# A diffusion step in fp32: the gate rows summed in four chunks, and a first modulation block of two tiles

## The chip, the core and the metric

One core of one Trainium2 chip runs the whole program. The metric is the device time of one execution in microseconds; the runs shown are three executions, and one further execution was taken by the hardware profiler. All times inside the kernel are from that profiled execution, counted from its first instruction.

## The reference

One layer of a trunk on 5 tiles of 128 tokens: one tile of context (the prompt), four of latent tokens. All in float32, D_MODEL = 2048.

```python
mod = silu(cond) @ w_ada + b_ada                 # 2048 x 6144, for two conditions: latent, context
shift, scale, gate = split(mod, 3)
h = rms_norm(x, g_norm) * (1 + scale) + shift
z = h @ w_in                                     # q, k, v, gates of both mixers
oa = diff_attention(...)                         # 8 heads: softmax 1 - lam * softmax 2
ob = gqa_attention(...)                          # 8 query heads on 2 key/value heads
o = concat(rms_norm(oa, subln) * silu(ga), ob * silu(gb)) @ w_out
x = x + gate * o
y = rms_norm(x, g_final)                         # also out: new keys and values of the context
```

The three thirds of w_ada are 16 MB each. Shift and scale are needed before the first projection, gate only after the last one.

## The kernel before

Products run on TensorE in float32 split into a high and a low part (fp32r): each 128 x 512 product is three matmuls, high x high, low weight x high, high weight x low (lines 588 to 590). A step is one block of 128 rows of a weight times the five token tiles, fifteen matmuls into the five banks of z_ps. Sixteen steps are a pass, which yields 512 output columns for all tokens. There are 17 passes: pass 0 for the keys and values of the grouped mixer (KV), passes 1 to 4 (G_IT on) for two grouped query heads each, passes 5 to 12 (D_IT on) for one differential head each, passes 13 to 16 (OUT_IT on) for w_out. Between the tiles of a pass stand pieces of the attention of the group that the pass before projected: QK transposes, scores S, transposes T of the probabilities, products V, transposes O of the output (STEPS, pieces_at). They use three PSUM banks, `ring`.

Weights arrive in w_raw (two pairs of row blocks), ScalarE copies them to w_hi, VectorE makes w_lo (split_w, line 1189) three steps ahead of TensorE. VectorE works in the order of its own program: in each step first split_w, then the attention's parts, and at the end of the step what belongs to the gate. TensorE waits for w_lo, and, for V and S, for pt_lo (line 1291), which frees or completes the probabilities. In the output passes VectorE multiplies z_ps by the gate rows (gated_y), adds x (add_x) and weighs by g_final (weight_y); the last pass finishes tile by tile.

Modulation. Shift and scale come in blocks of tiles of 128 columns, ADA_TILES. A block of n tiles is loaded in 2n loads of 1 MB into a ring of six buffers (ada_raw); a buffer is reloaded when its matmuls are done. TensorE multiplies each load by the conditions (modulation, line 610, sixteen or thirty-two small matmuls), VectorE copies the rows (modulation_rows), TensorE transposes them (columns, line 625), and VectorE makes the factors (modulation_columns). Block 0 comes before pass 0, the others between the tiles of pass 0 in slots given by ada_pieces: five slots a step. Step s of pass 0 needs the factors of tile s.

The gate third is not multiplied on TensorE as a matrix. VectorE forms sums over the sixteen row blocks of w_ada, weighted per partition (gate_sums, line 1390: acc = raw * cs + acc, for two conditions), and one small matmul group per 512 columns then adds over the partitions (step_gate, line 812). VectorE adds b_ada (gate_rows_out), GpSimd stores the rows to DRAM and loads them back, broadcast to 128 partitions, as gate_b for each output pass. The sums are 64 pieces of two instructions on 512 columns, ten a pass in passes 6 to 12:

```python
GATE_STEPS = [4, 4, 9, 9, 11, 11, 13, 13, 13, 13]
```

The group of matmuls follows step 0 of pass 13, the stores its step 3, and gate_b is loaded with x_add at step 10 of pass 13 and at step 1 of passes 14 to 16. Order is kept by semaphores alone; each engine's instructions stand in the order in which its function issues them.

## Time and profile before

| | us |
|---|---|
| median of the 3 runs shown | 1325.59 (1324.25 to 1325.9) |
| the profiled execution | 1323.39 |
| its span, first to last instruction | 1321.6 |
| TensorE busy | 1249.9 |
| VectorE busy | 799.8 |
| ScalarE busy | 607.0 |
| GpSimd busy | 245.0 |
| DMA | 156.54 MB |

The first matmul of pass 0 starts at 50.05, and the last instructions end 11 us after TensorE. Over the first 120 us the DMA engines are full, afterwards they move about 100 GB/s. The mean granted clock of TensorE is 0.991 of full speed; the share of a single stretch is in the rows. A busy share near one does not say that TensorE runs at its peak: matmuls overlap, and at the lower clock they are as busy and slower. So the waits and the clock of single stretches are to be read, not the share.

### The profile page before, as it was taken

Reading aid. Unit: us, or ns where it says so; the run is one execution under the profiler, and the core shown is the slowest. Engines: PE = TensorE matmul, PEld = TensorE weight load, DVE = VectorE, ACT = ScalarE, POOL = GpSimd, SP = SyncE. Lnnn points to the kernel's source line nnn. Section 1 sums busy time; section 2 is a strip of 40 time slices with the busy share of each in tenths; the row PEclk is TensorE's granted clock in tenths of the full one; section 3 lists DMA queues with packets and bytes.
Section 4 is the critical chain, followed back from the end, with each engine's and each line's share of the span. In section 5 each row is a group of like instructions: output and inputs, shape, how many; then the busy total and the mean of one; then the engine's idle time right before and its main releaser. Section 6 shows DMA issues by size and latency. Waiting matters only on the chain.

```text
span 1321.6 us, 18198 instructions
## 1 busy us (share of the span) xinstructions
PE 1249.9 (95%) x6903; PEld 1009.5 (76%) x6903; DVE 799.8 (61%) x1283; ACT 607.0 (46%) x1275; POOL 245.0 (19%) x426
## 2 busy tenths in 40 slices
PE   3899999999999999999999999999999899999996
PEld 1456778888888888887777787777777777888885
DVE  3344637657466565676767767677777776523343
ACT  4223325545545464464545445454545656322123
POOL 2010102002020040222222222222223232200001
PEclk9899999999999999999999999999999999999999
DMA  9998422112121121334243242323334331433234
GB/s 352 386 376 258 104 65 74 38 49 84 49 68 49 48 93 48 106 87 125 77 127 98 81 120 78 110 83 121 98 95 139 104 101 64 151 120 135 80 136 160
DMA packets 130904, 156.54 MB, mean 118 GB/s; under 512 B 8008, under 2 KB 98216, under 8 KB 130048
## 3 DMA queue, kind: packets, MB, share of 16 engines
q1 hardware_dynamic: 118032, 111.22, 25.7%
q0 software_dynamic: 12784, 44.15, 10.5%
q8 instruction: 55, 0.90, 0.3%
q14 instruction: 33, 0.27, 0.1%
HBM read 144.18 MB, written 11.16 MB: 118 GB/s over the span
## 4 chain that ended last, share of the span: by engine, by line
PE 81%; DVE 10%; ACT 2%; issue 2%; DMA 2%; POOL 1%; SPq 0%; ACTq 0%; DVEq 0%; POOLq 0%
PE z_ps L588 21%; PE z_ps L590 20%; PE z_ps L589 20%; PE ring L786 4%; PE ring L685 4%; DVE gate_acc L1390 3%; PE ring L720 3%; PE ring L610 2%; PE ring L788 2%; DVE w_lo L1189 1%; DMA ada_raw<-in_w_ada_dram 1%; DVE pt_lo L1291 1%; PE ring L590 1%; PE ring L589 1%; PE ring L588 1%
## 5 line engine op out<-in xcount | busy, mean ns | idle before, releaser
L588 PE MATMUL z_ps<-w_hi,xt_hi 128*128 128x512 f32 x1360 | 564.8, 415 | 8.4 <-DVE xt_lo L1183 7.4
L590 PE MATMUL z_ps<-w_hi,xt_lo 128*128 128x512 f32 x1360 | 533.6, 392 | 0.0
L589 PE MATMUL z_ps<-w_lo,xt_hi 128*128 128x512 f32 x1360 | 533.0, 392 | 0.0
L860 ACT ACTIVATE w_hi<-w_raw 128x512 fp32r<-128x512 f32 x272 | 170.5, 628 | 349.4 <-PE z_ps L590 338.4
L1189 DVE TENSOR_TENSOR w_lo<-w_raw,w_hi 128x512 fp32r<-128x512 f32 x272 | 191.5, 706 | 225.7 <-ACT w_hi L860 223.7
L588 PEld LDWEIGHTS z_ps<-w_hi,xt_hi 128*128 128x128 f32 x1360 | 257.0, 189 | 66.3 <-issue 20.8
L590 PEld LDWEIGHTS z_ps<-w_hi,xt_lo 128*128 128x128 f32 x1360 | 256.6, 189 | 57.0
L589 PEld LDWEIGHTS z_ps<-w_lo,xt_hi 128*128 128x128 f32 x1360 | 258.1, 190 | 39.3
L786 PE MATMUL ring<-v_hl,pt_hi 128*128 128x256 f32 x400 | 96.8, 326 | 14.8 <-DVE pt_lo L1291 13.9
L1266 DVE TENSOR_REDUCE small<-s_sb 128x2 f32<-128x1536 f32 (+1 forms) x60 | 87.9, 1466 | 23.5 <-ACT s_sb L860 22.6
L860 ACT ACTIVATE o_sum<-ring 128x128 f32<-128x128 f32 (+1 forms) x60 | 18.8, 314 | 178.2 <-PE ring L788 178.2
L967 ACT ACTIVATE s_sb<-s_sb,small 128x768 f32<-128x768 f32 (+1 forms) x120 | 97.9, 819 | 2.5 <-DVE small L1266 2.4
L786 PEld LDWEIGHTS ring<-v_hl,pt_hi 128*128 128x128 f32 x400 | 75.2, 188 | 20.5 <-issue 17.6
L788 PE MATMUL ring<-v_hl,pt_lo 128*128 128x128 f32 x400 | 89.1, 223 | 0.0
L860 ACT ACTIVATE pt_hi<-ring 128x256 fp32r<-128x256 f32 (+2 forms) x144 | 66.6, 467 | 47.0 <-PE ring L685 45.9
L1560 POOL TENSOR_TENSOR sg<-sg,zs 128x128 f32<-128x128 f32 (+1 forms) x60 | 36.6, 610 | 276.4 <-DVE sg L1249 275.8
L1291 DVE TENSOR_TENSOR pt_lo<-ring,pt_hi 128x256 fp32r<-128x256 f32 (+2 forms) x144 | 73.2, 523 | 21.4 <-ACT pt_hi L860 18.9
L1390 DVE SCALAR_TENSOR_TENSOR gate_acc<-gate_raw,cs,gate_acc 128x512 f32<-128x512 f32 x120 | 83.6, 761 | 0.2 <-issue 0.2
L788 PEld LDWEIGHTS ring<-v_hl,pt_lo 128*128 128x128 f32 x400 | 76.4, 191 | 2.8
L1302 DVE TENSOR_TENSOR o_sum<-ring,o_sum 128x128 f32<-128x128 f32 (+1 forms) x60 | 20.0, 333 | 87.1 <-ACT o_sum L860 87.1
L1249 DVE RECIPROCAL sg<-sg 128x128 f32<-128x128 f32 (+1 forms) x60 | 72.5, 1209 | 0.0
L685 PE MATMUL ring<-ident,s_sb 128*128 128x128 f32 x400 | 66.3, 272 | 0.0
(154 smaller groups left out, 1310.5 us busy)
## 6 DMA issues: line engine op xcount, KB each, us to landing
w_raw<-in_w_in_dram SPq DMA_DIRECT2D x192, 256.0 KB, 3.2
ada_raw<-in_w_ada_dram SPq DMA_DIRECT2D x64, 512.0 KB, 11.7
gate_raw<-in_w_ada_dram POOLq DMA_DIRECT2D x32, 512.0 KB, 4.7
w_raw<-in_w_out_dram SPq DMA_DIRECT2D x64, 256.0 KB, 3.5
o_spill<-row_st POOLq DMA_DIRECT2D x14, 320.0 KB, 3.1
row_st<-o_spill POOLq DMA_DIRECT2D x14, 320.0 KB, 3.4
x_sb<-in_x_sample_dram SPq DMA_DIRECT2D x4, 1024.0 KB, 10.2
w_raw<-in_w_in_dram POOLq DMA_DIRECT2D x16, 256.0 KB, 6.4
```

Source lines behind the costliest of these rows:

```text
L588: pe.matmul(out, hi_l, hi_r, start=start, stop=False)
L589: pe.matmul(out, hi_l, lo_r, start=False, stop=False)
L590: return pe.matmul(out, lo_l, hi_r, start=False, stop=stop)
L685: return pe.transpose(bank[:, col:col + P], src, ident[:, :])
L786: pe.matmul(bank[:, o:o + 2 * DH], pt_hi[c_][:, keys], v_hl[vh][:, vt, :], start=(j == 0), stop=False, skip_group_check=True)
L788: ins = pe.matmul(bank[:, o:o + DH], pt_lo[c_][:, keys], v_hl[vh][:, vt, 0:DH], start=False, stop=(j == tiles[-1][0]), skip_group_check=True)
L860: return act.activation(out, in_, ACT.Copy, **kw)
L967: act.activation(row, row, ACT.Exp, bias=nmax[:, t, c_:c_ + 1], accum_out=den[:, t, c_:c_ + 1]).then_inc(exp_done, 1)
L1189: dve.tensor_tensor(w_lo[:, b, :], w_raw[:, kg // 2 % RAW_RING, kg % 2, :], w_hi[:, b, :].bitcast(F32), ALU.subtract).then_inc(w_lo_done, 1)
L1266: dve.tensor_reduce(nmax[:, t, :], s_sb[:, t % 2, :, 0:(NKEY if t else P)], AX_X, ALU.max, negate=True).then_inc(max_ready, 1)
L1291: ins = dve.tensor_tensor(pt_lo[c_][:, keys], RB(n)[:, col:col + P * w], pt_hi[c_][:, keys].bitcast(F32), ALU.subtract)
L1390: ins = dve.scalar_tensor_tensor(acc, raw, weight, acc, ALU.mult, ALU.add)
```

## The change

Three things change.

1. The gate's columns are cut in four chunks of 512, one per output pass. Chunk 0 is summed in pass 1 (steps 4 to 7 and 9 to 12), chunks 1 to 3 in the output pass that ends with them, passes 14 to 16 (steps 1 to 5 and 7 to 9). A step takes two row blocks, four instructions on 512 columns. The raw rows come in loads of 512 KB for chunk 0 and 1 MB for the others, in two buffers each. Every chunk has its own group of small matmuls (now on 128 columns), adds, stores and broadcast: chunk 0 at steps 0 to 3 of pass 2, the others at steps 10 to 12 of their pass. Nothing of the gate is left in passes 5 to 13 but the load of gate_b for chunk 0. The eight loads of b_ada move from pass 5 to pass 1, and the computation of lambda (minus_lambda) from step 8 to step 13 of pass 1.
2. ADA_TILES is 2, 4, 4, 4, 2 instead of 4, 4, 4, 2, 2. Four loads come before pass 0 instead of eight, and 28 groups of matmuls lie in pass 0 instead of 24.
3. The columns of a block are transposed one slot earlier, and VectorE makes its factors in the step in which it copies the rows, a step earlier than before.

```diff
-GATE_COLS = D_MODEL // 2
-GATE_LOADS = 2 * KT
-GATE_STEPS = [4, 4, 9, 9, 11, 11, 13, 13, 13, 13]
-GATE_FROM = 4
-GATE_SUM_IT = OUT_IT
-ADA_TILES = [4, 4, 4, 2, 2]
+GATE_EARLY = [4, 5, 6, 7, 9, 10, 11, 12]
+GATE_LATE = [1, 2, 3, 4, 5, 7, 8, 9]
+ADA_TILES = [2, 4, 4, 4, 2]
...
-def gate_parts():
-    out, i = {}, 0
-    for it in range(D_IT + 1, GATE_SUM_IT):
-        for s in GATE_STEPS:
-            if i < 2 * GATE_LOADS and (it, s) >= (D_IT + 1, GATE_FROM):
-                out.setdefault((it, s), []).append(i)
-                i += 1
-    return out
-GATE_PARTS = gate_parts()
+def gate_steps(cc):
+    return G_IT if cc == 0 else OUT_IT + cc, GATE_EARLY if cc == 0 else GATE_LATE
+def gate_unit(cc, k):
+    n = 2 if cc == 0 else 4
+    return (k // n if cc == 0 else KT // 2 + (cc - 1) * (KT // 4) + k // n), n
+GATE_SUMS, GATE_SUM_AT, GATE_ROWS_AT, GATE_OUT_AT, GATE_LOADS = {}, {}, {}, {}, {}
+for _cc in range(OUTS):
+    _it, _steps = gate_steps(_cc)
+    for _i, _s in enumerate(_steps):
+        GATE_SUMS[(_it, _s)] = (_cc, _i)
+    _n = gate_unit(_cc, 0)[1]
+    for _q in range(KT // _n):
+        _s = _steps[(_q - 1) * _n // 2 - 1] + 1 if _q >= 2 else 2 if _cc == 0 else 0
+        GATE_LOADS.setdefault((_it, _s), []).append((_cc, _q))
+    GATE_SUM_AT[(G_IT + 1, 0) if _cc == 0 else (_it, 10)] = _cc
+    GATE_ROWS_AT[(G_IT + 1, 0) if _cc == 0 else (_it, 11)] = _cc
+    GATE_OUT_AT[(G_IT + 1, 3) if _cc == 0 else (_it, 11)] = _cc
...
-            i = (e + 1) * (slots - 6) // ADA_LOADS[c] - 1
+            i = max((e + 1) * (slots - 8) // ADA_LOADS[c] - 1, 0)
             out.setdefault(divmod(TILES * ADA_FIRST[c - 1] + i, TILES), []).append(("ADA", c, e))
-        out.setdefault(divmod(TILES * ADA_FIRST[c] - 5, TILES), []).append(("COLS", c, 0))
+        out.setdefault(divmod(TILES * ADA_FIRST[c] - 6, TILES), []).append(("COLS", c, 0))
...
-    gate_raw, e = place("gate_raw", [P, 2, GATE_COLS], F32, half0)
-    gate_acc, e = place("gate_acc", [P, 2, D_MODEL], F32, e)
-    gate_sel, e = place("gate_sel", [P, 2, 2], F32, e)
...
+    gate_raw0, e0 = place("gate_raw0", [P, 2, 2, NCOL], F32, e)
+    gate_acc0, e0 = place("gate_acc0", [P, 2, NCOL], F32, e0)
...
+    gate_raw1, e0 = place("gate_raw1", [P, 2, 4, NCOL], F32, e0)
+    gate_acc1, e0 = place("gate_acc1", [P, 2, NCOL], F32, e0)
...
-            def step_gate():
-                n = TURN["GATE"]
+            def step_gate(cc):
+                n = TURN[("GATE", cc)]
                 bank = claim(n)
                 pe.wait_ge(sel_set, 4)
-                pe.wait_ge(gate_summed, 2 * GATE_LOADS)
+                pe.wait_ge(gate_summed, KT * (cc + 1))
+                acc = gate_acc1 if cc else gate_acc0
                 for r in range(2):
                     for j in range(4):
-                        ins = pe.matmul(bank[32 * j:32 * j + 2, :], gate_sel[:, r, :],
-                                        gate_acc[:, r, NCOL * j:NCOL * (j + 1)], start=(r == 0), stop=(r == 1))
+                        ins = pe.matmul(bank[32 * j:32 * j + 2, 0:P], gate_sel[:, r, :], acc[:, r, P * j:P * (j + 1)],
+                                        start=(r == 0), stop=(r == 1))
                 filled(ins, n)
             for e in range(2):
                 modulation(0, e)
             for g in range(HT_GROUPS):
                 h_transposes(g)
-                modulation(0, 2 + g)
-            for e in range(2 + HT_GROUPS, ADA_LOADS[0]):
-                modulation(0, e)
+                if g < 2:
+                    modulation(0, 2 + g)
             columns(0)
...
+                if a == G_IT:
+                    wait_full(act, TURN[("GATE", 0)])
...
-                    if it == G_IT and s == KT // 2:
+                    if it == G_IT and s == KT - 3:
...
-            def gate_sums(i):
-                m, piece = divmod(i, 2)
-                k, u = divmod(m, 2)
-                dve.wait_ge(gate_in[u], 16 * (k + 1))
-                if k:
-                    dve.wait_ge(gate_summed, i - 3)
-                raw = gate_raw[:, u, NCOL * piece:NCOL * (piece + 1)]
-                c0 = GATE_COLS * u + NCOL * piece
-                for r in range(2):
-                    acc, weight = gate_acc[:, r, c0:c0 + NCOL], cs[:, KT * r + k:KT * r + k + 1]
-                    if k == 0:
-                        ins = dve.tensor_scalar(acc, raw, weight, None, ALU.mult)
-                    else:
-                        ins = dve.scalar_tensor_tensor(acc, raw, weight, acc, ALU.mult, ALU.add)
-                ins.then_inc(gate_summed, 1)
+            def gate_sums(cc, i):
+                for k in (2 * i, 2 * i + 1):
+                    g, n = gate_unit(cc, k)
+                    raw, acc = (gate_raw1, gate_acc1) if cc else (gate_raw0, gate_acc0)
+                    dve.wait_ge(gate_in[g % 2], 16 * (g // 2 + 1))
+                    if k:
+                        dve.wait_ge(gate_summed, KT * cc + k)
+                    elif cc:
+                        wait_full(dve, TURN[("GATE", cc - 1)])
+                    for r in range(2):
+                        src, weight = raw[:, g % 2, k % n, :], cs[:, KT * r + k:KT * r + k + 1]
+                        if k == 0:
+                            ins = dve.tensor_scalar(acc[:, r, :], src, weight, None, ALU.mult)
+                        else:
+                            ins = dve.scalar_tensor_tensor(acc[:, r, :], src, weight, acc[:, r, :], ALU.mult, ALU.add)
+                    ins.then_inc(gate_summed, 1)
...
-                        if s + 1 in ADA_FIRST:
-                            modulation_columns(ADA_FIRST.index(s + 1))
                         split_h(s + 1)
                         if s + 2 in ADA_FIRST:
                             modulation_rows(ADA_FIRST.index(s + 2))
+                            modulation_columns(ADA_FIRST.index(s + 2))
...
-                    if (it, s) == (GATE_SUM_IT, 1):
-                        gate_rows_out()
-                    for i in GATE_PARTS.get((it, s), []):
-                        gate_sums(i)
+                    if (it, s) in GATE_SUMS:
+                        gate_sums(*GATE_SUMS[(it, s)])
+                    if (it, s) in GATE_ROWS_AT:
+                        gate_rows_out(GATE_ROWS_AT[(it, s)])
...
+            def load_gate_rows(cc):
+                pool.wait_ge(gate_out, 64 * (cc + 1))
+                if cc:
+                    pool.wait_ge(y_add, TILES * cc)
                 for r in range(2):
-                    pool.dma_start(gate_b[:, r, :], gate_rows[r:r + 1, cols].broadcast_to([P, NCOL])
+                    pool.dma_start(gate_b[:, r, :], gate_rows[r:r + 1, NCOL * cc:NCOL * (cc + 1)].broadcast_to([P, NCOL])
                                    ).then_inc(gate_b_in, 16)
-            def load_gate(m):
-                k, u = divmod(m, 2)
-                c0 = 2 * D_MODEL + GATE_COLS * u
-                pool.dma_start(gate_raw[:, u, :], ada_v[k, :, c0:c0 + GATE_COLS]).then_inc(gate_in[u], 16)
-            def gate_begin():
-                pool.wait_ge(og_ready, OG_DONE[D_IT - 1])
-                for m in range(2):
-                    load_gate(m)
-                for r in range(2):
-                    pool.memset(gate_sel[:, r, r:r + 1], 1.0).then_inc(sel_set, 1)
-                    pool.memset(gate_sel[:, r, 1 - r:2 - r], 0.0).then_inc(sel_set, 1)
+            def load_gate(cc, q):
+                g, n = gate_unit(cc, (2 if cc == 0 else 4) * q)
+                if (cc, q) == (0, 0):
+                    for r in range(2):
+                        pool.memset(gate_sel[:, r, r:r + 1], 1.0).then_inc(sel_set, 1)
+                        pool.memset(gate_sel[:, r, 1 - r:2 - r], 0.0).then_inc(sel_set, 1)
+                if (cc, q) == (1, 0):
+                    for u in range(2):
+                        wait_full(pool, TURN[("O", OUT_IT - 1, 0)] + u)
+                if q >= 2:
+                    pool.wait_ge(gate_summed, KT * cc + n * (q - 1))
+                elif cc:
+                    pool.wait_ge(gate_summed, KT * cc)
+                c0 = 2 * D_MODEL + NCOL * cc
+                pool.dma_start((gate_raw1 if cc else gate_raw0)[:, g % 2, :, :], ada_p[:, n * q:n * (q + 1), c0:c0 + NCOL]
+                               ).then_inc(gate_in[g % 2], 16)
...
-                    if (it, s) == (D_IT, 4):
+                    if (it, s) == (G_IT, 4):
+                        pool.wait_ge(qk_ready, G_IT)
+                        bias = b_ada[:, 2 * D_MODEL:].rearrange("a (c j n) -> a c j n", c=OUTS, j=4)
                         for j in range(4):
                             for r in range(2):
-                                c0 = 2 * D_MODEL + 512 * j
-                                pool.dma_start(ada_rows[32 * j + r:32 * j + r + 1, :], b_ada[:, c0:c0 + 512]
-                                               ).then_inc(gate_bias, 16)
-                    if (it, s) == (GATE_SUM_IT, 3):
-                        wait_free(pool, TURN["GATE"])
+                                pool.dma_start(ada_rows[32 * j + r:32 * j + r + 1, :].rearrange("p (c n) -> p c n", c=OUTS),
+                                               bias[:, :, j, :]).then_inc(gate_bias, 16)
+                    if (it, s) in GATE_LOADS:
+                        for cc, q in GATE_LOADS[(it, s)]:
+                            load_gate(cc, q)
+                    if (it, s) in GATE_OUT_AT:
+                        cc = GATE_OUT_AT[(it, s)]
+                        wait_free(pool, TURN[("GATE", cc)])
                         for j in range(4):
-                            pool.dma_start(gate_rows[:, 512 * j:512 * (j + 1)], ada_rows[32 * j:32 * j + 2, :]
+                            c0 = NCOL * cc + P * j
+                            pool.dma_start(gate_rows[:, c0:c0 + P], ada_rows[32 * j:32 * j + 2, P * cc:P * (cc + 1)]
                                            ).then_inc(gate_out, 16)
...
                     if it == OUT_IT and s == 10:
-                        pool.wait_ge(gate_out, 64)
                         load_out_operands(0)
+                        load_gate_rows(0)
...
+                    if it > OUT_IT and s == 12:
+                        load_gate_rows(it - OUT_IT)
```

At TensorE's start (names: ada_raw holds w_ada, x_sb the normalized x, z_ps the projection) stood, before:

```order
L638 MATMUL ring<-ident,x_sb 128x128 x16
L644 MATMUL ring<-ident,x_sb 128x128 x4
L610 MATMUL ring<-ada_raw,cs 2x256 x24
L625 MATMUL ring<-ident,ada_rows 128x128 x2
L588 MATMUL z_ps<-w_hi,xt_hi 128x512
L589 MATMUL z_ps<-w_lo,xt_hi 128x512
L590 MATMUL z_ps<-w_hi,xt_lo 128x512
L610 MATMUL ring<-ada_raw,cs 2x256 x8
```

and stands now:

```order
L649 MATMUL ring<-ident,x_sb 128x128 x16
L655 MATMUL ring<-ident,x_sb 128x128 x4
L636 MATMUL ring<-ident,ada_rows 128x128
L599 MATMUL z_ps<-w_hi,xt_hi 128x512
L600 MATMUL z_ps<-w_lo,xt_hi 128x512
L601 MATMUL z_ps<-w_hi,xt_lo 128x512
L621 MATMUL ring<-ada_raw,cs 2x256 x56
L599 MATMUL z_ps<-w_hi,xt_hi 128x512
L600 MATMUL z_ps<-w_lo,xt_hi 128x512
L601 MATMUL z_ps<-w_hi,xt_lo 128x512
L621 MATMUL ring<-ada_raw,cs 2x256 x8
```

Block 0 ends with the transposes and one transpose of its rows; all of block 1 but one load follows the first tile of step 0.

On VectorE, at step 13 of pass 7 (pt_lo is what the V matmuls of TensorE wait for), stood, before:

```order
L1189 TENSOR_TENSOR w_lo<-w_raw,w_hi 128x512
L1302 TENSOR_TENSOR o_sum<-ring,o_sum 128x128
L1390 SCALAR_TENSOR_TENSOR gate_acc<-gate_raw,cs,gate_acc 128x512 x8
L1189 TENSOR_TENSOR w_lo<-w_raw,w_hi 128x512
L1291 TENSOR_TENSOR pt_lo_64<-ring,pt_hi_63 128x512
L1291 TENSOR_TENSOR pt_lo_64<-ring,pt_hi_63 128x256
L1319 SCALAR_TENSOR_TENSOR og<-o_sum,small,sg 128x128
L1189 TENSOR_TENSOR w_lo<-w_raw,w_hi 128x512
```

and stands now:

```order
L1203 TENSOR_TENSOR w_lo<-w_raw,w_hi 128x512
L1316 TENSOR_TENSOR o_sum<-ring,o_sum 128x128
L1203 TENSOR_TENSOR w_lo<-w_raw,w_hi 128x512
L1305 TENSOR_TENSOR pt_lo_64<-ring,pt_hi_63 128x512
L1305 TENSOR_TENSOR pt_lo_64<-ring,pt_hi_63 128x256
L1333 SCALAR_TENSOR_TENSOR og<-o_sum,small,sg 128x128
L1203 TENSOR_TENSOR w_lo<-w_raw,w_hi 128x512
```

The eight sums between o_sum and the next split weight are gone; nothing took their place.

On VectorE in pass 1, from step 4 to the k_lo of step 8 (gate_acc_84 and gate_raw_83 are chunk 0's), stood, before:

```order
L1189 TENSOR_TENSOR w_lo<-w_raw,w_hi 128x512 x6
L1162 TENSOR_TENSOR lam_raw_72<-lam_raw_72 128x512
L1162 TENSOR_TENSOR lam_raw_73<-lam_raw_73 128x512
L1164 TENSOR_REDUCE lam<-lam_raw_72 128x8
L1164 TENSOR_REDUCE lam<-lam_raw_73 128x8
L1171 TENSOR_TENSOR lam<-lam 128x8
L1172 TENSOR_SCALAR lam<-lam 128x8
L1257 TENSOR_TENSOR k_lo_61<-ring,k_hi_60 128x512
L1257 TENSOR_TENSOR k_lo_68<-ring,k_hi_67 128x512
```

and stands now:

```order
L1203 TENSOR_TENSOR w_lo<-w_raw,w_hi 128x512 x2
L1404 TENSOR_SCALAR gate_acc_84<-gate_raw_83,cs 128x512 x2
L1406 SCALAR_TENSOR_TENSOR gate_acc_84<-gate_raw_83,cs,gate_acc_84 128x512 x2
L1203 TENSOR_TENSOR w_lo<-w_raw,w_hi 128x512
L1406 SCALAR_TENSOR_TENSOR gate_acc_84<-gate_raw_83,cs,gate_acc_84 128x512 x4
L1203 TENSOR_TENSOR w_lo<-w_raw,w_hi 128x512
L1406 SCALAR_TENSOR_TENSOR gate_acc_84<-gate_raw_83,cs,gate_acc_84 128x512 x4
L1203 TENSOR_TENSOR w_lo<-w_raw,w_hi 128x512
L1406 SCALAR_TENSOR_TENSOR gate_acc_84<-gate_raw_83,cs,gate_acc_84 128x512 x4
L1203 TENSOR_TENSOR w_lo<-w_raw,w_hi 128x512
L1271 TENSOR_TENSOR k_lo_61<-ring,k_hi_60 128x512
L1271 TENSOR_TENSOR k_lo_68<-ring,k_hi_67 128x512
```

The lambda work ahead of k_lo has gone to step 13, and sixteen sums stand ahead of it instead, four after each split weight.

## Rows read from the trace of the kernel before

**Rows 1.** The page's part 1: engine, busy us (share of the span) xinstructions.
```profile
...
PE 1249.9 (95%) x6903; PEld 1009.5 (76%) x6903; DVE 799.8 (61%) x1283; ACT 607.0 (46%) x1275; POOL 245.0 (19%) x426
...
```

**Rows 2.** Waits of TensorE, passes 6 to 12: total us, times, longest.
```profile
...
PE ring L786 <- DVE pt_lo L1291: 13.9, 6, 2.5
PE ring L720 <- DVE pt_lo L1291: 8.2, 6, 3.2
PE ring L786 <- ACT s_sb L860: 0.9, 1, 0.9
```

**Rows 3.** Timeline of VectorE, passes 7, 12: start us, us, instruction [idle before].
```profile
...
675.27 5.38 DVE L1390 SCALAR_TENSOR_TENSOR gate_acc<-gate_raw,cs,gate_acc 128x512 f32<-128x512 f32 x8
...
681.17 1.01 DVE L1291 TENSOR_TENSOR pt_lo<-ring,pt_hi 128x512 fp32r<-128x512 f32 x2
...
1040.66 2.73 DVE L1390 SCALAR_TENSOR_TENSOR gate_acc<-gate_raw,cs,gate_acc 128x512 f32<-128x512 f32 x4
...
```

**Rows 4.** TensorE by stretch: length, busy us (xinstructions), granted clock, DMA share, GB/s.
```profile
...
682.00:688.00 6.00, 5.56 (x23) 0.72 0.74 229
759.00:765.00 6.00, 5.28 (x29) 1.00 0.78 235
...
```

**Rows 5.** Waits of TensorE in passes 0 and 1.
```profile
...
PE z_ps L588 <- DVE xt_lo L1183: 3.9, 4, 1.1
PE ring L685 <- DVE k_lo L1257: 2.9, 1, 2.9
...
```

**Rows 6.** Timeline of TensorE around the gate step of pass 13.
```profile
...
1074.01 1.90 PE L812 MATMUL ring<-gate_acc,gate_sel 128*2 128x512 f32 x16
...
```

**Rows 7.** Timeline of all engines at the start.
```profile
...
5.19 109.82 SPq L554 DMA_DIRECT2D ada_raw<-in_w_ada_dram  x64
...
41.37 2.89 PE L610 MATMUL ring<-ada_raw,cs 128*2 128x256 f32 x48
...
44.34 1.72 DVE L1124 COPY ada_rows<-ring 2x256 f32<-2x256 f32 x4 [0.36 <-PE ring L610]
...
50.05 0.77 PE L588 MATMUL z_ps<-w_hi,xt_hi 128*128 128x512 f32 x1 [3.44 <-DVE xt_lo L1183]
...
61.14 1.05 PE L610 MATMUL ring<-ada_raw,cs 128*2 128x256 f32 x16
...
```

**Rows 8.** Instructions on ada_raw up to 130 us; DMA from issue to landing.
```profile
...
L610 PE MATMUL ring<-ada_raw,cs x632: 272/379/634, 20.5 to 130.0; 128*2 128x256 f32 x96, 128*2 128x128 f32 x62
...
DMA to landing us min/median/max: 7.8/11.7/16.2
```

**Rows 9.** Timeline of VectorE in pass 14.
```profile
...
1175.11 0.69 DVE L1189 TENSOR_TENSOR w_lo<-w_raw,w_hi 128x512 fp32r<-128x512 f32 x1 [2.71 <-ACT w_hi L860]
```

**Rows 10.** Timeline of VectorE at step 8 of pass 1.
```profile
...
171.69 1.41 DVE L1162 TENSOR_TENSOR lam_raw<-lam_raw 128x512 f32<-128x512 f32 x2
...
175.38 1.29 DVE L1257 TENSOR_TENSOR k_lo<-ring,k_hi 128x512 fp32r<-128x512 f32 x2 [0.18 <-ACT k_hi L860]
...
```

**Rows 11.** Instructions on gate_raw: DMA from issue to landing.
```profile
...
DMA to landing us min/median/max: 3.8/4.7/6.8
```

**Rows 12.** Timelines of ScalarE and VectorE at the end.
```profile
...
1293.44 0.63 ACT L860 ACTIVATE w_hi<-w_raw 128x512 fp32r<-128x512 f32 x1 [2.77 <-PE z_ps L590]
...
1299.61 0.69 DVE L1353 TENSOR_TENSOR y_sb<-z_ps,gate_b 128x512 f32<-128x512 f32 x1 [1.40 <-PE z_ps L590]
...
1312.46 3.02 ACT L860 ACTIVATE y_sb<-y_sb,stat 128x1536 f32<-128x1536 f32 x2
...
```

**Rows 13.** DMA issues: engine op xcount, KB each, median us to landing.
```profile
...
w_raw<-in_w_in_dram SPq DMA_DIRECT2D x192, 256.0 KB, 3.2
...
gate_rows<-ada_rows POOLq DMA_DIRECT2D x4, 4.0 KB, 3.1
...
```

**Rows 14.** Instructions on lam_raw: DMA from issue to landing.
```profile
...
DMA to landing us min/median/max: 4.1/6.0/7.2
```

**Rows 15.** Waits of TensorE from pass 13 on.
```profile
...
PE ring L720 <- DVE pt_lo L1291: 0.4, 1, 0.4
```

35 lines of the change are left out of this document (15 added, 20 removed).

## The prediction, written before the changed kernel was run

> **What bounds the kernel now.** I read the page first, then the waits of TensorE, then the timelines around each wait. TensorE is busy 1249.9 of 1321.6 us [rows 1], so time can only be won where it starts late, waits or runs at the lower clock. In the stretch of passes 6 to 12 it waits 13.9 us in six places at line 786 and 8.2 us in six places at line 720, always for VectorE's pt_lo, and 0.9 us once for ScalarE [rows 2]. In front of that pt_lo VectorE's timeline shows the gate sums: 5.38 us for the eight at step 13, 2.73 us for the four at step 9 [rows 3]. The clock comes on top: after the wait at 682 the six microseconds have a granted clock of 0.72, after the equal wait at 760 it is 1.00 [rows 4]; 0.72 means that part of the stretch ran at the lower of the two levels, 1.2 instead of 2.4 GHz. The windows at 835 and 1045 read like the one at 682, those at 606, 912 and 988 like the one at 759. Each low window costs 6 x 0.28 = 1.7 us. In passes 0 and 1 the waits are 3.9 us (four, at the first tile of each modulation block) and 2.9 us (one, for k_lo) [rows 5].
>
> **The differential passes.** All gate sums leave passes 6 to 12. The six waits at line 786: ahead of the pt_lo at 681.17 stood 5.38 us of sums; TensorE waited 2.3 us, so VectorE is now ready 3 us early and the wait is gone: -13.9. At line 720 the usual wait is 1.0 us against 2.7 us of sums, gone too. The longest, 3.2 us in pass 12, has 2.73 us of sums before it [rows 3], and 0.5 us stay: -7.7. Of the 0.9 us for ScalarE I count 0.4, since it comes after a chain that also held sums. The three low-clock windows follow such waits and go with them: -5.1. Sum -27.1. Bounds: -28.1 if all goes, -11 if ScalarE or another wait takes half the places. What is late next is ScalarE's pt_hi, but pt_lo is held by the sums in VectorE's own order, not by it. The bias loads leave pass 5 and their 2 KB cost nothing at either place.
>
> **The gate step.** One group of sixteen records on 512 columns took 1.90 us on TensorE [rows 6]. Now there are four on 128 columns; the nearest row, 16 records of 256 columns, took 1.05 us [rows 7]. Half of that and a change of operands give 0.7 us each, 2.8 us together: +0.9. Bounds +0.2 (0.5 each) and +2.3 (1.05 each).
>
> **Start and pass 0.** The same 32 modulation groups run, but 28 instead of 24 lie inside pass 0. (a) The first matmul at 50.05 follows the last transposes, three split weights, the rows' copy and the columns; the three groups at 41.37 ran beside VectorE's work, not ahead of it [rows 7]. Only one group between the transposes (about 1 us) and half of the copies leave the path: -1.4, not the 4.2 us of four groups. (b) Four more groups in the pass: seven now stand in a row in the first slot (1.0 us each), the other 21 cost 1.05 us and a change of operands, some 1.2: 32.2 us against 24 x 1.2 = 28.8: +3.4. (c) VectorE computes the columns one step earlier, so the waits at the blocks' first tiles, 3.9 us [rows 5], go; the transposes of the rows keep theirs: -3.6. Sum -1.6. Against it stands the ring of six loads: loads 10 and 11 are issued only once the first groups of block 1 have run, at about 51 and 53 us, and loads take at least 7.8 us to land in this crowd [rows 8], less when the queue has run dry. Block 1's last group is due at about 60, so I expect no wait, and at the end there is room: the last issue is at 115.0, the last group at 130.0 [rows 7, 8]. Bounds -5 and +6 (two loads that land 3 us late, each time at the lower clock).
>
> **Pass 1.** VectorE gets 32 sums there. Two rows of w_ada cost 2.73 us [rows 3] and the wait on the sum just before, some 0.1 each: 2.9; with a split weight's 0.6 that is 3.5 us per step, and a step of TensorE takes 3.4 (a w_lo of 0.69 us and 2.71 us idle to the next, [rows 9]). The split weights are made three steps ahead, 10 us of cover, so being 1 us behind costs nothing. It matters only at step 8, where TensorE waits 2.9 us for k_lo [rows 5]: before, the lambda work (from 171.69 to 175.2) stood in front of k_lo at 175.38 [rows 10]. It moves to step 13, where nothing waits. In its place VectorE comes late from steps 4 to 7: the third and fourth pairs of w_ada rows are loaded only once the first two are summed, 4.7 us from issue to landing [rows 11] against the 3.5 us until they are wanted, so each such round loses about 1 us. I get k_lo at 175.7 on the old scale: +0.5. GpSimd's queue meets eight bias loads there, ahead of the third load; they are through before the first sum. Bounds -2.5 and +5. In pass 2 the four adds for the gate rows come before q_lo, some 0.3 us each (copies of twice the width took 1.72 us for four [rows 7]); q_lo waits for ScalarE in part, so +0.3.
>
> **The output passes.** There VectorE gets 32 sums in each of three. It starts step 1 with ten operations on y just done (0.6 to 0.7 us each, [rows 12]), needs 3.5 us a step for nine steps (at step 6 the weighing of y stands in place of sums), and is some 5 us behind all along. The split weights, at the head of each step, are then about 2 us later than now, of 10. The gate step of step 10 needs the last sum at about 1 us before TensorE gets there. Loads of 1 MB are issued a pass ahead or two steps ahead. So 0, bounds 0 and +6 (2 us at each gate step).
>
> **The tail.** Before, the last gate rows were in SBUF well before they were wanted. Now chunk 3 is summed in pass 16 itself, and its chain starts when TensorE has done step 10, at T = 1293.4 on the old scale [rows 12]: gate step 0.7; split weight and four adds to T+2.5; four stores of 0.5 us each, the last issued at T+4.2 and landed 3.1 us later [rows 13], T+7.3; then two broadcasts of 256 KB, 0.5 us apart. Four of that shape, for lam_raw, landed after 4.1 to 7.2 us, median 6.0 [rows 14]; for the second of two I take 5.5: T+13.4. But since TensorE finishes the last pass tile by tile, its first tile is ready at T+6.2 (1299.61) [rows 12]. VectorE therefore starts 6.5 us late and catches up while ScalarE becomes the chain: per tile 0.8 us of squares and 1.5 us of scaling (3.02 for two [rows 12]), 5 x 2.3 = 11.5 us after T+14.8, and about 0.5 us of waits: T+26.8. Now it ends at 1315.48 = T+22.1. That is +4.7, of which 0.7 is the gate step's: +4.0. Bounds 0 and +7.
>
> The Trainium skill, "DMA: Bandwidth & Descriptors" (section "Anatomy of one DMA — SWDGE (gpsimd) path"), prices one DMA at a fixed 2.0 us and its bytes at 436 GB/s, thus 2.6 us for 256 KB. By that rule the last gate rows would be there at T+10.5 and the tail would cost +1.1 instead of +4.0. This case's broadcasts of the same shape took 4.1 us at least and 6.0 us in the median [rows 14], so the measurement decides.
>
> **Sum.** -27.1 + 0.9 - 1.6 + 0.5 + 0.3 + 0 + 4.0 = -23.0. The profiled execution took 1323.4 us (span 1321.6), so 1300.4; the median of the runs shown, 1325.6, is 2.2 us above it, and on that scale I forecast 1302.6 us.
>
> **Rivals.**
> Cheap tail: the last broadcasts, alone on the queues, land in about 3 us, as plain loads of 256 KB do (3.2 us, [rows 13]). For it: lam_raw's four went beside other transfers. Then the sum is -25.9, 1299.7 us. This is what the skill's rule above would make of it. Chance 0.17.
> Starved start: with four groups' worth of loads consumed and the ring full, the DMA queues idle until TensorE reaches block 1, and later groups wait for their loads, in a pass in which loads are issued up to 115.0 and take 7.8 to 16.2 us to land [rows 7, 8]. Some 6 us more: about 1309. Against it: the last group has 7 us in hand. Chance 0.13.
> Half the waits stay: something else is as late as the sums, 22.1 + 5.1 us of waits and clock shrink only by half: +13, 1316. Against it: the equal steps of pass 13, without sums, have only one wait for pt_lo, of 0.4 us [rows 15]. Chance 0.08.
> The other side: VectorE as the new bound. In pass 1 and passes 14 to 16 it works 3.5 us in a step of 3.4, and two loads in flight serve two units of sums. If the loads come late, TensorE first uses up the 10 us of cover and then waits in every step, and its clock falls as at 682. With steps of s us a pass loses 8 (s - 3.4) - 10 us: as slow as before from s = 5.4 on (4 x 6 = 24 us). Steps of 6 us, landings of 9 us in pass 1 as in the crowd of pass 0 [rows 8], would cost 4 x 10.8 us and some 8 us of clock: about 1354. Against it: gate loads have landed in 3.8 to 6.8 us [rows 11]. Chance 0.04.
> The change doesn't do what it says: a gate chunk reaches its pass late, so that the gated y of passes 14 to 16 waits at each pass start, 3 x 3 us: 1312. Against it: there T+13.4 meets a first tile at T+15.0 (gate step 0.7, four steps of 3.4, a tile of 0.7), 1.6 us of room in each pass. Chance 0.06.
>
> **How the numbers follow.** The forecast itself has 0.52. Its own bounds and the cheap tail reach down to 1295; the starved start and the late chunk reach up to 1312; half of the waits staying and VectorE as the bound are left out, about 0.12, and the rest of the 2 in 10 are sizes beyond both ends. A measurement tells 0.2%, 2.7 us, from no change. Only VectorE as the bound is slower by that: slower 0.04. Within 0.2% lie 0.02, the part of the half-waits case in which the start is starved too and the tail dear; faster 0.94.
>
> **What would show it.** No waits of TensorE for pt_lo over 0.6 us in passes 6 to 12 and a granted clock of 1.00 throughout them: the main term. The first matmul near 48.6 and pass 1 starting within 2 us of before: the start. One wait of about 3 us for k_lo in pass 1. No wait at the gate steps of the output passes. In the tail, the first gated y some 13 us after TensorE's step 10, waiting for gate_b, and ScalarE without a gap after it. The forecast is wrong if pt_lo still waits for ScalarE, if weights (w_lo) hold TensorE in passes 1 or 14 to 16, or if waits for ada_raw appear in pass 0.

## The result, and the profile of the changed kernel

The changed kernel takes 1309.86 us in the median of 4 runs (1309.45 to 1312.91), the kernel before 1325.52 beside it: ratio 0.9888, interval 0.9871 to 0.9906, 15.7 us faster. Forecast were 23 us and 1302.6 us; 1309.9 lies in the range, near its upper end. The profiled execution took 1309.45 us, its span is 1307.7, and it is 13.9 us shorter than the profiled execution of before.

I cut both profiled executions at the first matmul of each pass. The differences are the terms of the prediction (passes 3 to 5 took 250.6 us both times):

| stretch | before, us | after, us | change | predicted |
|---|---|---|---|---|
| up to the first matmul of pass 1 | 142.95 | 145.04 | +2.1 | -1.6 |
| pass 1 | 59.09 | 64.36 | +5.3 | +0.5 |
| pass 2 | 82.31 | 83.09 | +0.8 | +0.3, a gate step of 0.7 |
| passes 6 to 12 | 535.57 | 508.57 | -27.0 | -27.1 |
| pass 13 | 76.47 | 74.49 | -2.0 | -1.9 |
| pass 14 | 54.40 | 56.76 | +2.4 | a gate step of 0.7 |
| passes 15 and 16 | 108.96 | 110.52 | +1.6 | gate steps of 1.4 |
| after the last matmul | 11.25 | 14.2 | +3.0 | +4.0 |

The page's part 1, which answers [rows 1]: TensorE's busy time hardly moved; what was won were waits and slow matmuls.

```profile
PE 1247.1 (95%) x6951; PEld 1009.8 (77%) x6951; DVE 808.6 (62%) x1295; ACT 606.1 (46%) x1275; POOL 250.0 (19%) x426
```

TensorE's waits in the whole span (us in total, times, longest), those that the prediction's steps touch; the one for xt_lo is of pass 13 and stood there before, too. Against [rows 2] the 22.1 us for pt_lo in passes 6 to 12 have shrunk to 2.0, both in pass 12 and the longer of them 1.7 us (the 2.3 here hold 0.4 of pass 13, as in [rows 15]). Against [rows 5] the waits for xt_lo at the blocks' first tiles are gone, the one for k_lo went from 2.9 to 6.4 us, and there are seven waits for ada_raw beside the long one at the start. Six of them lie inside pass 0, 5.2 us in all, where there was none:

```profile
PE ring L621 <- DMA ada_raw<-in_w_ada_dram: 22.5, 8, 16.3
PE ring L696 <- DVE k_lo L1271: 6.4, 1, 6.4
...
PE ring L731 <- DVE pt_lo L1305: 2.3, 3, 1.7
PE ring L824 <- DVE gate_acc L1406: 1.5, 1, 1.5
PE z_ps L599 <- DVE xt_lo L1344: 1.0, 1, 1.0
```

TensorE by stretch (length, busy, granted clock, DMA share, GB/s). Where [rows 4] had a clock of 0.72 it is 1.00 now:

```profile
682.00:688.00 6.00, 6.00 (x33) 1.00 0.31 90
```

VectorE in pass 1, which answers [rows 10] (start, duration, what, idle before and its releaser). The first sums start late, for their load; another load is waited for at 177.53; the k_lo stands at the end of that line:

```profile
164.90 0.88 DVE L1404 TENSOR_SCALAR gate_acc<-gate_raw,cs 128x512 f32<-128x512 f32 x2 [1.10 <-DMA gate_raw<-in_w_ada_dram]
...
168.65 0.69 DVE L1203 TENSOR_TENSOR w_lo<-w_raw,w_hi 128x512 fp32r<-128x512 f32 x1 [1.33 <-ACT w_hi L871]
...
177.53 2.93 DVE L1406 SCALAR_TENSOR_TENSOR gate_acc<-gate_raw,cs,gate_acc 128x512 f32<-128x512 f32 x4 [1.30 <-DMA gate_raw<-in_w_ada_dram]
180.38 0.68 DVE L1203 TENSOR_TENSOR w_lo<-w_raw,w_hi 128x512 fp32r<-128x512 f32 x1
180.99 1.28 DVE L1271 TENSOR_TENSOR k_lo<-ring,k_hi 128x512 fp32r<-128x512 f32 x2
```

The DMA engines in that stretch, and TensorE's clock behind the wait (columns PE, PEld, DVE, ACT, POOL busy, then clock, DMA share, GB/s). They are full from 157 to 164, and the wait costs twice, since matmuls then run in part at the lower level:

```profile
157.00:164.00 7.00, 7.00 (x32) 5.79 (x32) 6.73 (x12) 0.63 (x1) 5.67 (x15) 1.00 1.00 229
...
177.00:183.00 6.00, 1.28 (x5) 1.18 (x6) 4.62 (x7) 0.34 (x1) 0.72 (x1) 0.64 0.50 132
183.00:189.00 6.00, 6.00 (x24) 4.85 (x23) 3.51 (x6) 1.28 (x3) 0.00 (x0) 0.79 0.43 152
```

VectorE in the last pass, against [rows 12]: the first gated y waits 5.6 us for gate_b, 11.6 us after TensorE's step 10 (1275.3).

```profile
1277.02 1.18 DVE L1361 TENSOR_TENSOR ada_rows<-ring,ada_rows 2x128 f32<-2x128 f32 x4
...
1286.92 0.69 DVE L1368 TENSOR_TENSOR y_sb<-z_ps,gate_b 128x512 f32<-128x512 f32 x1 [5.62 <-DMA gate_b<-gate_rows]
```

### The profile page after: what moved, and what is told of

It is laid out like the page before. It is cut to its first block, busy times and chain, and to the rows that moved or that the text cites. A ratio compares the mean times of both kernels' runs of the same rounds, so it can differ in the third digit from the quotient of the medians.

```text
span 1307.7 us, 18319 instructions
## 1 busy us (share of the span) xinstructions
PE 1247.1 (95%) x6951; PEld 1009.8 (77%) x6951; DVE 808.6 (62%) x1295; ACT 606.1 (46%) x1275; POOL 250.0 (19%) x426
## 4 chain that ended last, share of the span: by engine, by line
PE 83%; DVE 6%; DMA 5%; SPq 2%; ACT 1%; issue 1%; POOL 1%; ACTq 0%; DVEq 0%; POOLq 0%
PE z_ps L599 22%; PE z_ps L601 21%; PE z_ps L600 21%; PE ring L696 5%; PE ring L797 5%; PE ring L731 3%; DMA ada_raw<-in_w_ada_dram 3%; PE ring L799 2%; DVE gate_acc L1406 2%; PE ring L621 1%; SPq L565 1%; PE ring L601 1%; PE ring L600 1%; PE ring L599 1%; DMA w_raw<-in_w_out_dram 1%
```

## The experiments

Each ran five rounds beside the kernel before, on the chip of its group of runs. "Changed" is the changed kernel; its ratio is 0.9888 in its first measurement and 0.9902 in the second, so kernels of different groups are compared by their ratios.

| kernel | median, us | before, us | ratio, interval |
|---|---|---|---|
| gate's change alone | 1309.39 | 1324.33 | 0.9881 (0.9868 to 0.9895) |
| start alone, in before | 1328.34 | 1324.33 | 1.0029 (1.0018 to 1.0041) |
| changed, old blocks | 1305.95 | 1324.33 | 0.9855 (0.9840 to 0.9870) |
| changed, sums after k | 1308.38 | 1324.33 | 0.9874 (0.9861 to 0.9888) |
| changed, again | 1312.84 | 1325.88 | 0.9902 (0.9888 to 0.9917) |
| changed, sums split | 1309.81 | 1325.88 | 0.9881 (0.9865 to 0.9897) |
| changed, x later | 1311.68 | 1325.88 | 0.9895 (0.9879 to 0.9912) |
| changed, group earlier | 1309.85 | 1325.88 | 0.9879 (0.9864 to 0.9894) |
| changed, all repairs | 1297.41 | 1324.88 | 0.9789 (0.9775 to 0.9802) |
| before, sums spread | 1298.12 | 1324.88 | 0.9795 (0.9781 to 0.9808) |
| before, three edits | 1289.32 | 1325.41 | 0.9727 (0.9712 to 0.9741) |
| changed, groups ahead | 1306.68 | 1325.41 | 0.9866 (0.9846 to 0.9885) |

### The start

**The gate's change alone.** In the changed kernel:

```diff
-ADA_TILES = [2, 4, 4, 4, 2]
+ADA_TILES = [4, 4, 4, 2, 2]
...
```

with the slots, the columns and the place of modulation_columns as before, too.

> The gate's four chunks as in the changed kernel, but the start of the kernel before (blocks of 4, 4, 4, 2, 2 tiles, columns as before). Theory, from the changed kernel's waits for ada_raw in pass 0 (5.2 us in six places) and its longer pass 0 (95.67 against 92.90 us, with a first matmul only 0.7 earlier): the first block of two tiles costs 2.1 us rather than saving anything, so this kernel starts pass 1 at 143 instead of 145 and takes 1309.9 - 2.1 = 1307.8 us. Rival, the prediction's own count (the start is worth -1.6, and what came in pass 0 is from the gate's moved DMAs or from another execution): 1309.9 + 1.6 = 1311.5 us.

**The start alone**: the same edit the other way round, in the kernel before.

> The kernel before with the changed kernel's start alone (blocks of 2, 4, 4, 4, 2 tiles, columns one step earlier); the gate sums stay in passes 6 to 12. Theory (the new start starves for loads): 1325.5 + 2.1 = 1327.6 us, pass 1 starting near 145 with the same six waits for ada_raw. Rival (the start is worth -1.6): 1323.9 us. In both, passes 6 to 12 keep their 22 us of waits for pt_lo.

**The old blocks with the early factors**: in the changed kernel ADA_TILES = [4, 4, 4, 2, 2] and its loop ahead of pass 0, nothing else.

> The changed kernel with blocks of 4, 4, 4, 2, 2 tiles again, but with its columns one slot and its factors one step earlier. Theory: the wait of 3.9 us at the blocks' first tiles was removed by the earlier factors, and the starvation came from the block of two tiles alone; then both are gone here: 3.5 to 4 us under the kernel with the gate's change alone, so about 1304 us, pass 0 about 89.5 us long. Rival: the loads set the length of pass 0 whatever the blocks (the last lands at 122 to 127 us), and the 3.9 us turn up as waits for ada_raw: then within 1 us of the kernel with the gate's change alone, 1307 to 1308 us.

Pass 1 starts at 142.2, 145.9 and 138.8 us in the three; in seven executions with the block of two behind its first tile it lies between 145.0 and 146.8. TensorE's waits up to pass 1 follow, the start alone first, then the gate alone, then the old blocks with early factors. The longest of each line (16 us for the first load, 3.4 us for the first xt_lo) lies ahead of pass 0. Inside pass 0 the start alone waits 5.4 us for ada_raw, the gate alone never, and the old blocks 1.3 us.

```profile
PE ring L610 <- DMA ada_raw<-in_w_ada_dram: 23.0, 7, 16.5
```

```profile
PE z_ps L599 <- DVE xt_lo L1198: 7.4, 5, 3.4
```

```profile
PE ring L621 <- DMA ada_raw<-in_w_ada_dram: 18.2, 3, 16.1
...
PE z_ps L599 <- DVE xt_lo L1198: 3.4, 1, 3.4
```

In the kernel before, the start costs 4.0 us of the whole time (0.29%), of which 2.9 are there when pass 1 starts; the theory's sign is right, its size was too small. In its profile pass 1 is another 1.6 us longer than before (60.7 against 59.1): the wait for k_lo is 2.9 us as before, but here the clock fell after it (the last section shows both). In the changed kernel I expected 1307.8 without it and measured 1309.4; its ratio is 0.07 and 0.21 points under the changed kernel's two, which no single comparison resolves. The second of the two was meant to test this: if the start costs 4 us here too, it had to come out 2 to 4 us above the gate's change alone, and 0.21 points are 2.8 us. The two halves of the start work against each other: the early factors save 3.5 us (142.2 to 138.8; four of the five waits for xt_lo gone), the block of two costs more than that: with it and the early factors pass 1 starts 6 to 8 us later than with the early factors alone, and the whole time is 0.33 to 0.47 points longer, 4 to 6 us.

**Three groups ahead**, in the changed kernel:

```diff
+            for e in range(3):
+                modulation(1, e)
             columns(0)
```

The three groups are left out of pass 0.

> The changed kernel with its block of two tiles, but with the first three groups of block 1 ahead of the transposes of block 0's rows, where TensorE waits 3.8 us for VectorE's copy, instead of behind the first tile of pass 0. Their data have landed by 37.1, 39.8 and 42.5 us. Theory (starved start): in the changed kernel loads 10 and later were issued only from 52.7 us on, after an idle stretch since 38.4, because their buffers were freed by groups that stood behind the first tile; now they are issued from about 43 us on, the DMA share in 40 to 60 us goes back over 1, the waits for ada_raw near 58 to 62 us go, and three groups of 1.1 us leave pass 0: pass 1 starts at 140 to 142 instead of 145 to 146.8, 1312.8 - 4 = 1306 to 1309 us. Rival: the loads are the limit over the whole pass (last landing at 127 us in any case) and later waits for ada_raw grow by what the first lose: pass 1 starts at 144 or later, 1311 us or more.

TensorE and the DMA engines in 50 to 60 us, changed and with the groups ahead (busy, clock, DMA share, GB/s):

```profile
50.00:60.00 10.00, 8.92 (x118) 0.88 0.77 268
```

```profile
50.00:60.00 10.00, 8.77 (x90) 0.83 1.04 385
```

The buffers are now reloaded from 43.6 us on instead of 52.7, the engines stay full, the last load lands at 123.7 instead of 126.9 (122.2 before), and pass 1 starts at 142.0. Three groups of about 1 us have also left pass 0, which alone could explain the 3.0 us won. It does not: in all eight executions with the block of two tiles, this one included, TensorE's last wait for ada_raw ends when load 26 lands (counted from 0, as below), and pass 1 starts 35.5 to 35.6 us after that wait. With the groups ahead that load lands at 106.4 instead of 109.5, and pass 1 starts 3.0 us earlier. So the loads set the length of pass 0, and the starved start is shown. What stays are waits for ada_raw of 1.2 us at 58 and of 3.0 us in three places around 100; against the old blocks with early factors (138.8) the block of two still costs 3 us.

### Pass 1

**The sums after k**, **the sums split**:

```diff
-GATE_EARLY = [4, 5, 6, 7, 9, 10, 11, 12]
+GATE_EARLY = [4, 9, 10, 11, 12, 13, 14, 15]
```

The second has [4, 5, 9, 10, 11, 12, 13, 14] there, and minus_lambda (with ScalarE's part) at step 15.

> The changed kernel with chunk 0's sums at steps 4 and 9 to 15 of pass 1 instead of 4 to 7 and 9 to 12, so that only one of eight steps of sums stands ahead of the k_lo of step 8. Theory: the 6.4 us wait for k_lo and the low clock behind it (granted 0.64 and 0.79 in 177 to 189, some 1.7 us) are VectorE's lateness from the sums, and with lambda gone from there too the wait falls under 1 us: 1309.9 - 7 = 1303 us. Rival: k_lo waits for ScalarE's k_hi or for the w_raw loads that land late beside the broadcasts for lambda; then 2.5 us or more of the wait stay, 1306 to 1307 us. A third: the last sums at step 15 make the gate step of pass 2 wait or w_lo late, some 2 us back.

> The changed kernel with chunk 0's sums at steps 4, 5 and 9 to 14 of pass 1, and the lambda work at step 15. Moving all but one step of sums behind the k_lo freed 8.4 us in pass 1, but the last sums at step 15 ended at 208.99 and TensorE's gate step of pass 2 waited for them, 4.2 us and the lower clock after it. Theory: with steps 6 and 7 free VectorE is on time for k_lo (it has w_lo made by 174.3, k_hi is ready at 174.5), and the sums end a step earlier, at 205.5, before the gate step is due: no wait at either place, pass 1 56 us and pass 2 near 83: 1309.9 - 8.3 + 0.3, about 1302 us. Rival: the lateness has only been moved; w_lo or the gate step waits around 205 to 210, 2 to 4 us come back, 1304 to 1306 us.

TensorE's only wait from 145 to 300 us in the one and in the other:

```profile
PE ring L824 <- DVE gate_acc L1406: 4.2, 1, 4.2
```

```profile
PE z_ps L599 <- ACT zs L871: 5.4, 1, 5.4
```

Both times k_lo was on time. Pass 1 fell to 56.0 us in the one, and in the other to 56.2 us and the 5.4 us that TensorE waits at its end. So the cause was the sums ahead of k_lo, with the loads for which they waited, and not k_hi. Both times most of it came back at the border to pass 2: first the third of my cases, the gate step waiting for sums at step 15 (pass 2: 89.9 us), then something neither theory had. ScalarE's program waits for lambda's sums before it copies z out of PSUM:

```profile
206.71 0.22 ACT L1071 ACTIVATE lam<-lam 128x16 f32<-128x16 f32 x1 [7.14 <-DVE lam L1178]
206.93 2.56 ACT L871 ACTIVATE zs<-z_ps 128x512 f32<-128x512 f32 x5
```

Passes 1 and 2 together took 145.9 and 146.6 us, against 147.5 and 148.3 in the changed kernel's two profiles and 141.4 before.

### Pass 14 and the tail

**x later**:

```diff
-                    if it > OUT_IT and s == 1:
+                    if it > OUT_IT and s == 9:
                         load_out_operands(it - OUT_IT)
```

> The changed kernel with the loads of x (1.25 MB for each of passes 14 to 16) issued at step 9 instead of step 1. In pass 14 they stand beside the first two loads of gate_raw (2 MB): DMA share 0.97 from 1126 to 1136, w_raw is late and VectorE idles 3.5 us at 1141 for w_hi, and the gate step then waits 1.5 us for the sums. Theory: apart, the loads of x cost nothing, VectorE does not idle there and the gate step's wait goes: 1.5 to 2.5 us less than the changed kernel, pass 14 near 55.2 us. Rival: two loads of gate_raw alone keep w_raw late, or VectorE has no room anyway (44 us of work in steps 0 to 10): the wait stays within 0.5 us and so does the time.

The changed kernel's VectorE had idled 3.5 us in pass 14, for ScalarE's w_hi; ScalarE's row shows what was late, its load of w_raw:

```profile
1140.95 0.69 DVE L1203 TENSOR_TENSOR w_lo<-w_raw,w_hi 128x512 fp32r<-128x512 f32 x1 [3.54 <-ACT w_hi L871]
```

```profile
1140.29 0.63 ACT L871 ACTIVATE w_hi<-w_raw 128x512 fp32r<-128x512 f32 x1 [5.83 <-DMA w_raw<-in_w_out_dram]
```

With x later there is no such gap, the gate step waits for nothing and pass 14 takes 55.18 us, as pass 15 does: the theory, in the trace. In the measured time it is 1.2 us (0.07 points), which is inside the intervals of both and shows nothing by itself.

**Group earlier**: GATE_LATE = [1, 2, 3, 4, 5, 6, 7, 8], weight_y at step 12 instead of 6, and step_gate, gate_rows_out, the stores and load_gate_rows one step earlier.

> The changed kernel with VectorE's weighing of y moved from step 6 to step 12 of passes 14 to 16, the gate sums at steps 1 to 8 without that gap, and gate step, adds, stores and broadcasts one step earlier each. Theory: the tail's 3.0 us are the lateness of gate_b (first gated y 11.6 us after TensorE's step 10, waiting for it); a step of 3.4 us earlier it waits for TensorE's first tile and little more: the time after the last matmul goes from 14.3 to 11.5 us or so, 2.5 to 3 us less in all. Rival: ScalarE's chain (0.8 us of squares and 1.5 us of scaling per tile) or the queue to GpSimd sets the end anyway, then at most 1 us is won. The other side: the gate step, now one step earlier, waits more for the sums, above all in pass 14 (1.5 us now): some 1 to 3 us lost there.

After the last matmul there are 11.4 us left, against 14.4 in the changed kernel beside it: the 3 us of the tail are the lateness of gate_b. The median is 3.0 us less, as the theory said, and the profiled execution 2.2 us. The latter is not for the theory's reason alone: 3.0 us came from the tail and 0.9 us from a start of pass 1 that was earlier in this execution, while passes 14 and 15 grew by 1.0 us each. What grew is a wait of 0.7 us at the start of passes 15 and 16 for the gated y, which stood behind a late w_lo in VectorE's order:

```profile
1183.79 0.69 DVE L1203 TENSOR_TENSOR w_lo<-w_raw,w_hi 128x512 fp32r<-128x512 f32 x1 [4.47 <-ACT w_hi L871]
1184.51 3.08 DVE L1368 TENSOR_TENSOR y_sb<-z_ps,gate_b 128x512 f32<-128x512 f32 x5
```

**All repairs** together, with the sums split and minus_lambda at step 6:

> All repairs together, in the changed kernel: blocks of 4, 4, 4, 2, 2 tiles with the columns early (3.5 us less to the start of pass 1 than the gate's change alone), the loads of x at step 9 (took pass 14 from 56.5 to 55.2 us), the gate groups of passes 14 to 16 a step earlier with the weighing of y at step 12 (took the tail after the last matmul from 14.5 to 11.4 us), and chunk 0's sums at steps 4, 5 and 9 to 14 of pass 1. With the lambda work at step 15 ScalarE held back its copies of z for it and TensorE waited 5.4 us at the start of pass 2; now the lambda work stands at step 6, where VectorE has 2.7 us idle a step. Theory: the parts are separate and add up. From 1305.9 for the blocks: pass 1 from 65.6 to 57 or 58 (k_lo perhaps 1 to 2 us late from lambda), pass 14 59.2 to 55.5, tail -3: ratio to the kernel before 0.975, 1291 to 1293 us. Rival: what is freed in one place turns up as a wait in the next (pass 2's gate step, w_raw beside the moved loads): half of it stays, 1297 to 1299 us.

The rival's number, 1297.4 us, 27.5 under before. Pass 0 (start of pass 1 at 137.7), pass 14's wait and the tail came as said. But pass 1 took 61.3 us, since lambda, now ahead of k_lo again and behind loads that came late, made TensorE wait 3.8 us, and passes 14 to 16 kept 1.7, 1.7 and 0.9 us over the length they had before.

### The differential passes

**Sums spread**, one line of the kernel before:

```diff
-GATE_STEPS = [4, 4, 9, 9, 11, 11, 13, 13, 13, 13]
+GATE_STEPS = [4, 4, 5, 7, 9, 11, 11, 13, 15, 15]
```

> The kernel before with one line changed: the gate sums of passes 6 to 12, ten pieces a pass as before, at steps 4, 4, 5, 7, 9, 11, 11, 13, 15, 15 instead of 4, 4, 9, 9, 11, 11, 13, 13, 13, 13. So 1.4 us of sums stand before the pt_lo of steps 10 and 14 instead of 2.7 and 5.4 us; the other pieces go where VectorE's timeline has idle time (4.0 us at step 15, 2.4 us at step 7). Theory: the 22 us of waits for pt_lo and the 5 us of low clock come from where the sums stood, not from how much VectorE has to do: nearly all of the 27 us goes without moving any sum to another pass, about 1300 us, passes 6 to 12 of 72.3 to 73 us. Rival: it is the amount (VectorE is busy 53 of 72 us there) and the sums make it late wherever they stand: half or more of the waits stay at other steps, 1311 us or more.

VectorE at step 13 and 15 of pass 7, to be read against [rows 3], and TensorE's waits in passes 6 to 12:

```profile
672.53 1.41 DVE L1390 SCALAR_TENSOR_TENSOR gate_acc<-gate_raw,cs,gate_acc 128x512 f32<-128x512 f32 x2
673.85 0.68 DVE L1189 TENSOR_TENSOR w_lo<-w_raw,w_hi 128x512 fp32r<-128x512 f32 x1
674.46 1.01 DVE L1291 TENSOR_TENSOR pt_lo<-ring,pt_hi 128x512 fp32r<-128x512 f32 x2
...
679.40 2.73 DVE L1390 SCALAR_TENSOR_TENSOR gate_acc<-gate_raw,cs,gate_acc 128x512 f32<-128x512 f32 x4
```

```profile
PE ring L720 <- DVE pt_lo L1291: 2.4, 3, 1.3
```

The same 128 sums in the same passes, and passes 6 to 11 take 72.3 to 72.9 us, as in the changed kernel, where there are none. Of the 27.0 us by which passes 6 to 12 became shorter in the changed kernel, 26.6 came here from the place of the sums alone. VectorE is as busy as before (799.4 us): it had the time, but 4 of 10 pieces stood in a row ahead of one pt_lo. The measured time says the same: 26.8 us less than the kernel before.

**Three edits**: the same line, the early factors and columns, and minus_lambda at step 13 (KT - 3) instead of 8; blocks, gate group and tail as before.

> The kernel before with three small edits and none of the gate's chunks: the sums spread within passes 6 to 12 as in the last comparison (worth 26.8 us there), the factors of a modulation block made one step and its columns one slot earlier (3.5 us in the changed kernel), and the lambda work at step 13 of pass 1 instead of step 8 (with sums nearly gone from before k_lo, that wait vanished). Theory: three separate terms, -26.8, -3.5 and -3 (the wait of 2.85 us and a little clock): 1325 - 33.3 = 1292 us, ratio 0.975; pass 0 near 88.5 us, pass 1 near 56. It has no tail and no gate steps in passes 14 to 16 to pay for, so it beats all kernels so far. Rival: in pass 1 the k_hi chain of ScalarE or the w_raw loads keep 2 us or more of the wait, and the loads of w_ada eat the early factors: 1296 us or more.

The expectation was 1292. It is 1289.3 us, 36 us or 2.7% under the kernel before, 1.6 points or 21 us under the changed one and the fastest of all. Pass 1 starts at 138.6 us and takes 56.0. TensorE does not wait in it. VectorE, against [rows 10], is idle until k_hi is there:

```profile
166.72 0.69 DVE L1189 TENSOR_TENSOR w_lo<-w_raw,w_hi 128x512 fp32r<-128x512 f32 x1 [2.71 <-ACT w_hi L860]
167.75 0.69 DVE L1257 TENSOR_TENSOR k_lo<-ring,k_hi 128x512 fp32r<-128x512 f32 x1 [0.34 <-ACT k_hi L860]
```

## Why the prediction was right, and where it was wrong

Over the profiled executions 13.9 us were won and 23.0 said. Of the 9.1 us between them 3.7 lie at the start, 4.8 in pass 1 and 1.7 in pass 14; the tail gave 1.0 back. Three things that the prediction said would not be seen were seen: waits for ada_raw in pass 0, a wait at a gate step of the output passes, and a wait for pt_lo over 0.6 us.

**Passes 6 to 12: right, to 0.1 us, in part by terms that cancel.** The six waits at line 786 and the low clock are gone, and with them the wait for ScalarE. At line 720 all are gone but 2.0 us in pass 12, where 0.5 was said: ahead of the pt_lo in question VectorE still has other work of its own, a reduction of 1.75 us among it. So 21.0 us of waits went instead of 22.0. The other 6.0 us, said as 5.1, are the three stretches at the lower clock (1.7 each) and 0.9 us that no wait shows. The rival that half the waits stay fell: nearly all of them were the sums' doing. What I did not ask is whether the sums had to leave the passes for that. They had not, and all that the change pays elsewhere (7 us in passes 1 and 14, three more gate steps, the tail) is the price of moving work that only had to be shifted by one or two steps.

**Pass 13 and the gate steps: right.** Each later gate step adds 0.78 us to its pass (0.7 said).

**Start: wrong sign.** The step that failed is the one after the sum of (a) to (c): "Block 1's last group is due at about 60, so I expect no wait". The groups ran as said, six in 6.06 us. Load 10 was therefore due for the seventh at 57.0, which the prediction did not look at, and load 11 for the last at 60.0. Issued at 52.7 to 54.2 us, they landed at 58.0 and 60.7, and TensorE waited 1.0 and 0.7 us. The prediction's own numbers, 51 and 53 us and at least 7.8 more, had given 58.8 and 60.8; "no wait" rested on the hope that loads land sooner on a queue that has run dry. They did (in 4.8 and 6.5 us), but were issued later. The larger part stood only in a rival and not in the forecast: the queue had begun no load between 38.4 and 52.7, and in a pass in which the loads are the limit this idle stretch shifts all later ones. The last lands 4.7 us later than before, and four more waits of 0.5 to 1.1 us come between 82 and 110. "At the end there is room" was true of the last load before and not of the ones in between. The rival "starved start" is what happened: pass 1 starts 3.7 us later than the forecast had it, and 4.5 us later in the start alone, where the rival had 6. The early factors were rightly valued (3.6 said, 3.5 measured), the first matmul came 0.7 instead of 1.4 us earlier.

**Pass 1: mis-sized**, +0.5 said, +5.3 measured. The term that failed is the landing times. I took 4.7 us from [rows 11], from passes where the DMA share is 0.35, and only for the third and fourth loads. Those landed after 4.0 and 5.0 us, and the fourth cost 1.3 us, as I had counted. The first load I took to be there in time. It was issued behind lambda's four broadcasts, with w_raw's loads and the bias beside it, landed after 7.5 us, and the first sums waited 1.1 us for it. In the same crowd w_raw took 7.1 us instead of 3.2 [rows 13], so that w_hi, and VectorE behind it, came 1.3 us late. TensorE's wait for k_lo is 3.5 us longer than before, and the low clock after the wait (0.64 and 0.79) makes the other 1.8, a term that I had counted for passes 6 to 12 and not here.

**Passes 14 to 16: "So 0" held for 15 and 16, not for 14 (+1.7 beside the gate step).** In pass 14 the loads of x, of g_final and of two gate units met, w_raw was late, VectorE idled 3.5 us, and the gate step waited 1.5 us. The gate step waits between 1.1 and 2.6 us in each of the eight executions in which x is loaded at step 1.

**Tail: +4.0 said, +3.0 measured**, by the mechanism described. The stores landed after 1.6 us instead of 3.1, the two broadcasts after 4.1 and 4.4 instead of 5.5. By the rule of the Trainium skill ("DMA: Bandwidth & Descriptors", section "Anatomy of one DMA — SWDGE (gpsimd) path") the estimate for a broadcast of 256 KB is 2.6 us; the measurement decides for the longer ones, here too.

The rival of the other side, VectorE as the new bound, is what pass 1 began to be, and pass 14 with 1.5 us; TensorE never waited for a w_lo.

## What to carry to other kernels

When TensorE waits for another engine, read that engine's timeline ahead of the awaited result: if work nobody is waiting for stands there, first shift it by a step or two into the idle time that the same timeline shows, before moving it to another phase. A landing time is worth only what the DMA share of its stretch is worth: price a moved load by the traffic of the place to which it goes. And where loads are the limit, what frees their buffers is part of the critical path, even when it looks like work that can wait.
